# All four slots of each expert's second matrix as a three-term product, two splits moved into the gate product, and a scatter that skips blank rows

## The reference, cut to what matters

```python
def moe_ffn(h, w_router, b_router, w_in, b_in, w_out, b_out):   # 512 tokens, 32 experts, top 4
    ...
    def expert_block(args):
        xb, e = args
        hcat = xb @ w_in[e] + b_in[e]                 # w_in[e]: 1024 x 2048
        x_glu = jnp.minimum(hcat[:, :D_FF_2], SWIGLU_LIMIT)
        x_lin = jnp.clip(hcat[:, D_FF_2:], -SWIGLU_LIMIT, SWIGLU_LIMIT)
        act = x_glu * jax.nn.sigmoid(SWIGLU_ALPHA * x_glu) * (x_lin + 1)
        return act @ w_out[e] + b_out[e]              # w_out[e]: 1024 x 1024
    ys = lax.map(expert_block, (xs, block_exp)).reshape(n_rows, dm)
    y = jax.ops.segment_sum(ys * row_gate[:, None].astype(ys.dtype), row_tok, num_segments=n + 1)[:n]
    return y.reshape(b, t, dm)
```

## Time and profile before

| | |
|---|---|
| median of 3 runs | 4421.21 us (4421.2 to 4421.22) |
| profiled execution | 4436.79 us, its span 4434.7 us |
| mean granted TensorE clock | 0.953 of full speed |
| busy over the span: PE, DVE, ACT, POOL | 4046.9, 2515.6, 1565.5, 119.0 us |
| moved by DMA | 660.38 MB |

### The profile page before, as it was taken

The page is one execution under the profiler, slowest core; times in us unless marked ns, Lnnn a source line. Parts: engine busy times, 40 slices in busy tenths (PEclk is TensorE's granted clock), DMA queues, the critical chain, the costliest instruction groups (busy, mean ns, idle before and its releaser), DMA issues.

```text
span 4434.7 us, 85713 instructions
## 1 busy us (share of the span) xinstructions
PE 4046.9 (91%) x37425; PEld 3087.9 (70%) x37425; DVE 2515.6 (57%) x3167; ACT 1565.5 (35%) x1923; POOL 119.0 (3%) x113
## 2 busy tenths in 40 slices
PE   7988998999999997898999889688799999999996
PEld 5867885688877876885687565344577777777774
DVE  5966773422323666774434210672577777777774
ACT  3243222200112253332101121452466566666652
POOL 0000000000000000000000000000200000000000
PEclk8989999999999998999999989898799999999998
DMA  5430001111122430001222224001599999999994
GB/s 227 156 114 4 4 5 69 48 67 65 59 72 86 157 143 31 4 4 58 78 95 95 97 98 148 8 1 53 221 350 352 353 356 356 354 356 354 355 358 145
DMA packets 114682, 660.38 MB, mean 149 GB/s; under 512 B 13488, under 2 KB 13488, under 8 KB 56528
## 3 DMA queue, kind: packets, MB, share of 16 engines
q1 hardware_dynamic: 101344, 610.74, 36.8%
q0 software_dynamic: 13024, 44.90, 3.8%
HBM read 637.68 MB, written 27.47 MB: 150 GB/s over the span
## 4 chain that ended last, share of the span: by engine, by line
PE 81%; DVE 11%; ACT 4%; issue 2%; DMA 2%; POOL 0%; SPq 0%; DVEq 0%; ACTq 0%; POOLq 0%
PE psum L790 53%; PE psum L1458 16%; PE psum L1484 5%; PE psum L1475 4%; DVE work L2168 1%; PE psum L1451 1%; DVE xt L1841 1%; DVE work L1873 1%; PE psum L1432 1%; PE psum L1442 1%; DVE work L1876 0%; POOL places L728 0%; DVE work L1801 0%; DMA xt<-x_wide 0%; DMA ring<-stream 0%
## 5 line engine op out<-in xcount | busy, mean ns | idle before, releaser
L790 PE MATMUL psum<-ht_parts,ahead_parts 128*128 128x512 f32 (+1 forms) x2016 | 673.0, 350 | 0.6 <-DVE ht_parts L2042 0.6
L790 PE MATMUL psum<-work 64*64 64x64 f32 (+3 forms) x12936 | 577.7, 243 | 93.6 <-ACT work L2567 25.9
L790 PEld LDWEIGHTS psum<-work 64*64 64x64 f32 (+2 forms) x12936 | 451.9, 139 | 183.4 <-issue 66.5
L790 PE MATMUL psum<-work_parts,ring_parts 128*128 128x512 f32 x1344 | 481.7, 359 | 0.0
L790 PE MATMUL psum<-work_parts,ahead_parts 128*128 128x512 f32 x1248 | 432.6, 358 | 10.2 <-ACT work_parts L2432 9.9
L790 PEld LDWEIGHTS psum<-ht_parts,ahead_parts 128*128 128x128 f32 (+1 forms) x2016 | 368.8, 185 | 60.2 <-DVE ring_parts L2035 1.4
L790 PE MATMUL psum<-ht,ring 128*128 128x512 f32 (+1 forms) x832 | 319.3, 545 | 8.1 <-DVE ht L2184 6.1
L790 PEld LDWEIGHTS psum<-work_parts,ring_parts 128*128 128x128 f32 x1344 | 254.4, 189 | 40.1
L790 PE MATMUL psum<-xt_parts,ahead_parts 128*128 128x512 f32 (+5 forms) x768 | 264.1, 345 | 16.1 <-ACT xt_parts L2432 12.0
L790 PEld LDWEIGHTS psum<-ht,ring 128*128 128x128 f32 x832 | 159.2, 192 | 166.2 <-issue 153.4
L1458 PE MATMUL psum<-work_parts 128*128 128x512 f32 x1024 | 273.7, 394 | 0.0
(11 more groups left out here) (323 smaller groups left out, 6938.1 us busy)
## 6 DMA issues: line engine op xcount, KB each, us to landing
ring<-stream SPq DMA_DIRECT2D x192, 1024.0 KB, 4.9
ring<-w_in SPq DMA_DIRECT2D x192, 1024.0 KB, 6.7
ht<-w_in SPq DMA_DIRECT2D x64, 1024.0 KB, 6.5
ht<-w_out SPq DMA_DIRECT2D x64, 1024.0 KB, 7.2
ring<-w_out SPq DMA_DIRECT2D x64, 1024.0 KB, 7.0
xt<-x_wide SPq DMA_DIRECT2D x8, 391.5 KB, 15.1
xt<-x_wide POOLq DMA_DIRECT2D x1, 3132.0 KB, 10.8
xt_rows<-xt POOLq DMA_DIRECT2D x8, 391.5 KB, 2.7
```

Of the source, the lines that this page charges most:

```text
L790: mm = pe.matmul(*args, **kwargs)
```

## The change

The second product uses the three terms for all four slots (`OUT_SPLIT = 4`), so DVE and ACT split twelve slots an expert. The activations are split over their whole width, in one instruction on each engine. The high parts get a sixth buffer, in the space of `htok`, with a wait for `htok`'s stores at its first use. DVE places split 10 behind its last read of the gate product and split 11 behind the activations; ACT places high part 10 ahead of the sigmoid and 11 behind it. The scatter gets the gather's bounds check, so that blank rows aren't written.

```diff
-EXPERT_RING, HIGHS = 6, 5
-OUT_SPLIT = 2
+EXPERT_RING, HIGHS = 6, 6
+OUT_SPLIT = 4
@@ carving of the buffers
+        htok_parts = work_parts[:, at[0] - TQ * DM:at[0]]
-        (e_act_high, e_act_high_r), e_act_low = carve_parts(DM), carve_parts(DM)[1]
+        e_act_high, e_act_low = carve_parts(DM)[1], carve_parts(DM)[1]
         highs = [ahead_parts, None, ht_low.rearrange("p k w -> p (k w)")[:, 2 * SLOT:3 * SLOT], y_bias_parts[:, 0:SLOT],
-                 y_bias_parts[:, SLOT:2 * SLOT]]
+                 y_bias_parts[:, SLOT:2 * SLOT], htok_parts[:, 0:SLOT]]
@@ gpsimd, scatter
-                pool.indirect_dma_start(sum_rows, tokens_of(n), y_sel, None, compute_op=ALU.add).then_inc(scattered, 16)
+                pool.indirect_dma_start(sum_rows, tokens_of(n), y_sel, None, bounds_check=SEQ - 1, oob_is_err=False,
+                                        compute_op=ALU.add).then_inc(scattered, 16)
@@ tensor, expert_out
-                        for k, (lhs, wt) in enumerate(((e_act_high_r, high), (e_act_high_r, low), (e_act_low, high))):
+                        for k, (lhs, wt) in enumerate(((e_act_high, high), (e_act_high, low), (e_act_low, high))):
                             for c in range(2):
-                                flush(pe.matmul(psum[:, 6 + c, :], lhs[:, a], wt[:, f, 512 * c:512 * c + 512],
-                                                start=(h == 0 and f == 0 and k == 0), stop=False))
-                    pending[0] += 1
-                for h in range(OUT_SPLIT, 4):
-                    n = eslot(r, e, j0 + h)[0]
-                    wt = raw_slots[n % EXPERT_RING].rearrange("p (f c) -> p f c", f=2)
-                    pe.wait_ge(*eslot_landed(r, e, j0 + h))
-                    for f in range(2):
-                        for c in range(2):
-                            mm = flush(pe.matmul(psum[:, 6 + c, :], e_act_high[:, P * (2 * h + f):P * (2 * h + f) + P], wt[:, f, 512 * c:512 * c + 512],
-                                                 start=False, stop=(h == 3 and f == 1)))
+                                mm = flush(pe.matmul(psum[:, 6 + c, :], lhs[:, a], wt[:, f, 512 * c:512 * c + 512],
+                                                     start=(h == 0 and f == 0 and k == 0), stop=(h == 3 and f == 1 and k == 2)))
                     pending[0] += 1
@@ vector, turn
-                    for j in range(2, KT if start else SPLIT_SLOTS):
+                    for j in range(2, KT if start else SPLIT_SLOTS - 2):
                         split_low(r, e, j)
...
                     if not last:
                         pick_expert(e + 1)
+                    if not start:
+                        split_low(r, e, SPLIT_SLOTS - 2)
                     stt(lin, lin, 1.0, glu, ALU.add, ALU.mult).then_inc(dve_chain, 1)
...
                     dve.wait_ge(act_ready, w.next(act_ready))
+                    if not start:
+                        split_low(r, e, SPLIT_SLOTS - 1)
                     if not last:
                         tokens_low()
@@ scalar, split_high and turn
+                if j == HIGHS - 1 and type(e) is int and e == 0:
+                    act.wait_ge(htok_out, 16 * TQ)
...
-                    for j in range(2, SPLIT_SLOTS if n else KT):
+                    for j in range(2, SPLIT_SLOTS - 1 if n else KT):
                         split_high(r, e, j)
                     sigmoid()
+                    if n:
+                        split_high(r, e, SPLIT_SLOTS - 1)
```

More of the change, by code:

```diff
@@ L2276, in act_low_part @@
                 dve.wait_ge(act_high_ready, w.next(act_high_ready))
-                n = 2 * P * OUT_SPLIT
-                tt(e_act_low[:, 0:n], psum[:, 4:6, :].rearrange("p b c -> p (b c)")[:, 0:n], e_act_high_r[:, 0:n].bitcast(F32), ALU.subtract
-                   ).then_inc(act_low_ready, 1)
+                tt(e_act_low, psum[:, 4:6, :].rearrange("p b c -> p (b c)"), e_act_high.bitcast(F32), ALU.subtract).then_inc(act_low_ready, 1)
             def pick_expert(e):
@@ L2866, in act_high_part @@
                 act.wait_ge(act_turned, w.next(act_turned))
[L2867 to L2870, removed]
+                fn(e_act_high, psum[:, 4:6, :].rearrange("p b c -> p (b c)"), ACT.Copy).then_inc(act_high_ready, 1)
             def sigmoid():
```

## The result

The changed kernel takes 4451.19 us, the median of 4 runs (4447.01 to 4461.84). The kernel before took 4421.22 beside it, so the ratio is 1.0069 with a 95% interval of 1.0057 to 1.0082: slower by 30 us. The prediction was 4410.4, its range 4396 to 4440. The profiled execution took 4461.84 us, the longest of the four, with a span of 4459.8; against the profiled execution of before its span is 25.1 us longer. The loop of experts accounts for more than that: from the first L1477 matmul of the second product (3204.2) to the one behind the loop (4386.9) there are 1182.7 us, where before had 1148.4 (3212.8 to 4361.2). That is 34.3 more; the stages ahead of the loop, which the change does not touch, took 8.6 less in this execution, and the tail 0.6 less.

What follows compares the result with a forecast made beforehand. PE was taken as the bound, with DMA only keeping pace. 0.26 us less an expert, times 31, gave 8.1; with 2.7 from the tail, 10.8 off the median 4421.21: 4410.4 us, range 4396 to 4440.

Steps and rivals of the forecast that it cites:

- the tail: Work behind the loop of experts: forecast 2.7 us shorter, 1.24 from the last expert's slots and 1.5 from its scatter.
- I take 1.2: In each expert, the halved scatter lets the w_out load of slot 9 land 1.2 us sooner.
- G = P−0.55: Forecast average over experts: the first gate instruction starts 0.55 us ahead of the second product's first matmul.
- G: Mark in each expert: start of the first gate instruction on DVE; forecast 0.55 us ahead of P.
- P: Mark in each expert's period: PE's first second-product matmul, where the previous expert's second matrix begins.
- −0.26 an expert: Saving in each expert's period: activation transposes at P+12.22 in place of P+12.48; times 31, 8.1 us.
- rival 1: Slot 9's landing comes no sooner: G at P+0.2, 0.49 us more an expert, 4434 us; chance 0.21.
- rival 2: PE's pause of 1 us in each expert lowers the clock: 1.7 us an expert, 4463 us; chance 0.10.
- The chain from G: DVE's gate work and splits 10 and 11 in each expert: fourth slot's products start at G+9.96 at the earliest.
- rival 4: A skipped scatter row costs what a written one does, so the scatter gets no shorter; counted under rival 1.
- Rival 3: PE waits for nothing, split 11 coming by P+8.43: 1.24 us kept 32 times, 4380 us; chance 0.05.
- The last scatter: Behind the loop, POOL waits 8.25 us for it before reading the sums; forecast 1.5 us less.

Runs made afterwards that it cites:

- e2: The kernel before with only the scatter's bounds check added: 4432.05 us, ratio 1.0004 to the kernel before.
- e12: The changed kernel with 12 transposes of a constant on PE ahead of its wait for split 11: 4449.03 us, ratio 1.004 to the kernel before.
- e8: The changed kernel with split 11 right behind split 10, ahead of the gate arithmetic: 4412.86 us, ratio 0.9961 to the kernel before.
- e5: The changed kernel with an expert's tokens spread over the 128 places: 4457.35 us, ratio 1.0064 to the kernel before.
- e1: The changed kernel with the old scatter, all 128 rows without bounds check: 4447.26 us, ratio 1.0044 to the kernel before.
- e10: The changed kernel with each gather replaced by a DMA of 1 KB, scatters kept: 4443.05 us in one run.
- e9: The changed kernel with each scatter replaced by a DMA of 1 KB, gathers kept: 4419.0 us in one run.
- e4: The changed kernel with every gather and scatter replaced by a plain DMA of 1 KB: 4412.71 us, ratio 0.9967 to the kernel before.
- e7: The changed kernel with three of four slots as three terms, the fourth raw fp32, no split 11: 4414.02 us, ratio 0.9964 to the kernel before.
- e3: The kernel before with one more two-operand DVE add of 2.3 us an expert, behind split 1: 4435.87 us in one run.

## Why the prediction was wrong

**What failed** is one term: "Removing 1.5 us of backlog shortens its landing by up to 1.5 [...] I take 1.2". It shortened by nothing: 7.32 to 7.47 us in e2, 7.32 to 7.62 with the whole change. With it fell "on average I take G = P−0.55"; G was P+0.41. That is 0.96 us an expert, 30 us over 31, and it turns the forecast's −0.26 an expert into +0.7. Of the 0.96, 0.76 is the relief that did not come (from the 0.21 of before to −0.55); the other 0.20, G later than before, is not explained, and single profiles differ by as much. This is rival 1, its mechanism and nearly its numbers: it gave the fourth slot P+10.16 and the transposes P+12.97, where e12, which has the same marks without the clock, shows 10.32 and 13.21. I gave it 0.21. Its time of 4434 is not reached, for two reasons: it left out the clock (rival 2), and the two together were in no rival and not in the range; and it took 2.7 us off the tail, which came out 0.6 shorter.

**Why relief of bytes gave no relief of time.** I had treated the software traffic as backlog in a queue that is always full, so that its length counts. Three runs contradict that. The delay does not add up (1.9 and 2.1 apart, 2.9 together); with the bytes halved it stays (e2); and in the changed kernel DMA moves less (337 GB/s, share 0.91 against 0.97), with time to spare that no load uses, since a load is issued only when PE frees a slot. What is shown is that the presence of a gather or scatter among an expert's loads delays slot 9 by about 2 us, and that halving the scatter's bytes hardly matters. Why was not settled. The packets of skipped rows remain (288 an expert), which would fit a price per packet, but no run took packets away without taking the transfer away.

**Rival 2, the clock,** came true in part, and it came on top of rival 1. The timeline of PE in the expert where the clock fell, with a pause of the same 1.76 us before it:

```profile
3363.20 1.09 PE L1477 MATMUL psum<-work_parts 128*128 128x512 f32 x4
...
3366.98 0.80 PE L1477 MATMUL psum<-work_parts 128*128 128x512 f32 x2 [1.76 <-DVE ring_parts L2265]
...
3368.43 1.91 PE L1477 MATMUL psum<-work_parts 128*128 128x512 f32 x4
...
3371.42 1.04 PE L1444 MATMUL psum<-con,work 128*128 128x128 f32 x8
```

Four matmuls took 1.09 us ahead of the pause and 1.91 behind it, near half the speed, that is 1.2 in place of 2.4 GHz; the granted clock of the stretch is 0.57. Seven experts of 31 had this, about 1.7 us each, 12 us in this execution; over all experts it is the 0.33 us between the 13.54 and the 13.21 of e12. My price of 1.7 was right. My reason for a small chance, "here everything around is dense", was no protection: the second idle of the earlier trace rows was the better witness. e12 shows the cause: with the pause filled and nothing else gained, the low clock is gone and the ratio goes from 1.0069 to 1.004, some 0.3%, 13 us. The Trainium skill (TensorE: Matmul & The Clock Gate, A second HAM failure mode: psum-queue depth-cycling) describes frequent short idles between groups of matmuls, with which the clock falls and recovers; here the trace agrees, in 7 of 31 cases.

**The sum by its steps.** An expert costs 38.78−37.65 = 1.13 us more: the forecast's −0.26, +0.96 from G, +0.33 from the clock, and 0.1 of small things. Times 30 it is 34 us, all that the loop lost.

**What was right.** The chain from G: the fourth slot at G+9.9 against 9.96 (split 10 at G+2.77, split 11 at G+7.57, both to the hundredth). The matmul counts and their 2.8 us a slot. One wait of PE for the split an expert. Little else became late: DVE had no wait for ACT's high part of slots 10 and 11, and its 88% fitted; only where G came at P+0.74 or later did PE wait a little for split 10 too, 0.4 us at most. The last product behind the loop took 13.5 us in place of 15.0, which is 1.5 less where I had 1.24. The software queue's share went as forecast, so rival 4 in its words (a skipped row costs what a written one does) is false; its outcome came all the same. Rival 3 did not come, and e8 shows that its price was wrong too: with PE hardly waiting in the second product, the period is 37.23 and not 36.4, since DVE, now behind by two splits, is late for the next gate product.

**What was wrong besides.** Two small readings were off: the wake-up of PE that the prediction calls about 0.1 us is 0.15 by its own row, and rival 3 asks DVE's chain to be 0.9 us shorter where its numbers give 0.98; neither moves the result. The last scatter gave nothing: POOL's wait before it loads the sums went from 8.25 to 8.07, where I took 1.5 off. The timeline of POOL behind the loop, and DMA around that scatter (4403 to 4412):

```profile
4402.31 1.56 POOL L757 DMA_INDIRECT sum_rows<-work  x1 [18.04 <-ACT work L2877]
4411.95 2.24 POOL L779 DMA_DIRECT2D work<-sum_rows  x4 [8.07 <-issue]
```

```profile
q0 software_dynamic: 144, 0.25, 18.8%
```

The engines' time for it did halve (18.8% of 9 us, 1.7, against 3.4), its wait did not. It is the same error a second time: I took the time that a transfer occupies for the time until it is done. The whole tail is 0.6 us shorter, where the sum had 2.7.

## What to carry to other kernels

A transfer's bytes and its share of the DMA engines say what it costs when it is the bound; the delay that it causes for a load behind it has to be measured by taking the transfer out, and cutting its bytes may change nothing. When work is added on an engine whose start hangs on a landing, put whatever TensorE wants first right behind that start and let work with slack (here the gate arithmetic) come after: one moved line made 1.0069 into 0.9961, and with the old scatter 0.9939. A pause that the new order leaves in TensorE costs more than its length where the clock falls behind it; to price it, fill it with idle work and compare.

## What the runs showed of the hardware

**Short pauses and the clock.** PE's idle time just ahead of the fourth slot was 1.6 us in the mean in the changed kernel, with 7 low experts; 1.5 us in e5, with 3; 1.4 us in e1, with 1; 1.2 us in e10, 1.1 in e9, 0.7 in e4 and 0.3 in e12, with 0. In all 11 low experts it was 1.76 or 1.77 us. The pause of 1.76 us left the clock at 1.00 in one expert and at 0.57 in the next, and of the changed kernel's 18 pauses of 1.74 us or more 7 were followed by a low clock and the others not, so the length alone does not decide.

**POOL beside DVE.** The view of groups over the loop, POOL alone (busy us, mean ns), of the kernel before, the changed one, e7 and e8:

```profile
L756 POOL DMA_INDIRECT sum_rows<-work x30 | 47.7, 1589 | 1054.5 <-ACT work L2883 1054.5
```

```profile
L757 POOL DMA_INDIRECT sum_rows<-work x30 | 66.9, 2231 | 1037.8 <-ACT work L2877 1005.0 <-issue 32.8
L748 POOL DMA_INDIRECT work<-htok_rows,work x29 | 62.3, 2150 | 8.8 <-issue 8.8
```

```profile
L757 POOL DMA_INDIRECT sum_rows<-work x31 | 50.1, 1616 | 1076.1 <-ACT work L2888 1006.8 <-issue 69.3
L748 POOL DMA_INDIRECT work<-htok_rows,work x29 | 32.3, 1114 | 8.8 <-issue 8.8
```

```profile
L757 POOL DMA_INDIRECT sum_rows<-work x31 | 74.7, 2408 | 1031.9 <-ACT work L2876 963.6 <-issue 68.3
```

In the mean the same instruction took 1.6 us where DVE had gaps and 2.2 to 2.4 where it ran splits without one; the gather's went from 1.0 to 2.2. One by one, the changed kernel's gathers took either 1.0 or 2.5 to 2.7 us. The Trainium skill (SBUF — State Buffer, SBUF: two separate sides) says that DVE with two SBUF inputs and a GpSimd operation that reads SBUF lock each other out of a shared port; the longer instructions fit that, and so does e3: an add with two SBUF inputs that ran 0.39 us into a scatter made that scatter 0.27 us longer, both times that it did. So that DVE's work slows POOL is shown in those two cases; that a shared port is the reason is not. It is not what made slot 9 late: e7 has the short POOL instructions and the same 7.63 us.
